# Where the stages of a two-layer encoder meet: splits, loads and waits by chunk and tile, and one pipeline across the turn

## The reference

```
h = rms_norm(x, norm_mix_pre[l]);  z = h @ w_in[l]              # 10 parts, 6144 columns
a = hgrn2_mixer(...);  b = diff_attention(...)                  # 512 columns each
m = sigmoid(gate_a) * (a @ w_branch_a[l]) + sigmoid(gate_b) * (b @ w_branch_b[l])
x = x + rms_norm(m @ w_out[l], norm_mix_post[l])
f = conv_ffn(rms_norm(x, norm_ffn_pre[l]), w_up[l], ...)        # 5632 columns up, 2816 down
x = x + rms_norm(f, norm_ffn_post[l])
x = x + rms_norm(sigmoid(rms_unit(x) @ w_ple_gate[l]) * (p[l] @ w_ple[l]), norm_ple[l])
```

## Time and profile before

| | |
|---|---|
| median of 3 runs | 2769.68 us |
| the profiled execution, its own time | 2770.27 us |
| its span | 2768.5 us |
| TensorE (PE) busy | 2635.0 us, 95% |
| VectorE (DVE), ScalarE (ACT), GpSimd (POOL) | 1478.4, 1063.6, 192.1 us |
| mean granted TensorE clock | 0.979 |

### The profile page before, as it was taken

The page is one execution under the profiler, slowest core; times in us unless marked ns, Lnnn a source line. Parts: engine busy times, 40 slices in busy tenths (PEclk is TensorE's granted clock), DMA queues, the critical chain, the costliest instruction groups (busy, mean ns, idle before and its releaser), DMA issues.

```text
span 2768.5 us, 36209 instructions
## 1 busy us (share of the span) xinstructions
PE 2635.0 (95%) x14994; PEld 2276.9 (82%) x14994; DVE 1478.4 (53%) x1836; ACT 1063.6 (38%) x1595; POOL 192.1 (7%) x272
## 2 busy tenths in 40 slices
PE   6999999999899999999979999999998999999998
PEld 5888988887688888887768889888776888888876
DVE  3166664444544444877442665743445444558774
ACT  3344453333332322455333544532333333234553
POOL 0001110000100000002111011100001000000021
PEclk9999999999899999999989999999998999999999
DMA  5534433344322222533235334333343222225321
GB/s 172 150 112 126 117 117 101 107 141 150 102 56 62 72 66 61 196 106 120 84 105 164 100 126 126 114 110 115 130 146 99 61 61 61 61 68 203 140 89 54
DMA packets 276222, 301.17 MB, mean 109 GB/s; under 512 B 9184, under 2 KB 210016, under 8 KB 276064
## 3 DMA queue, kind: packets, MB, share of 16 engines
q1 hardware_dynamic: 212192, 162.29, 19.6%
q10 hardware_dynamic: 63872, 136.64, 14.4%
HBM read 243.85 MB, written 55.05 MB: 108 GB/s over the span
## 4 chain that ended last, share of the span: by engine, by line
PE 87%; DVE 6%; ACT 3%; issue 2%; ACTq 1%; POOL 1%; DMA 0%; POOLq 0%; SPq 0%; DVEq 0%
PE ps L600 32%; PE ps L783 23%; PE ps L884 9%; PE ps L988 5%; PE ps L776 3%; PE ps L684 3%; PE ps L613 2%; PE ps L629 2%; PE ps L743 2%; PE ps L762 1%; PE ps L722 1%; PE ps L968 1%; PE ps L649 1%; PE ps L753 1%; DVE O L1231 1%
## 5 line engine op out<-in xcount | busy, mean ns | idle before, releaser
L600 PE MATMUL ps<-hT_hi,whi 128*128 128x256 f32 (+1 forms) x1664 | 428.0, 339 | 12.8 <-DVE hT_lo L1274 8.7
L600 PE MATMUL ps<-hT_hi,wlo 128*128 128x256 f32 (+1 forms) x1664 | 427.3, 338 | 0.0
L600 PE MATMUL ps<-hT_lo,whi 128*128 128x256 f32 (+1 forms) x1664 | 426.0, 337 | 0.0
L1061 DVE TENSOR_TENSOR wlo<-raw,whi 128x2048 fp32r<-128x2048 f32 x116 | 266.7, 2299 | 264.9 <-ACT whi L1559 264.9
L600 PEld LDWEIGHTS ps<-hT_hi,whi 128*128 128x128 f32 x1664 | 315.1, 190 | 50.5 <-issue 14.1
L600 PEld LDWEIGHTS ps<-hT_hi,wlo 128*128 128x128 f32 x1664 | 315.5, 190 | 37.3
L600 PEld LDWEIGHTS ps<-hT_lo,whi 128*128 128x128 f32 x1664 | 315.1, 189 | 37.0
L783 PE MATMUL ps<-hT_hi,whi 128*128 128x256 f32 (+1 forms) x1280 | 333.0, 342 | 5.0 <-ACT gst L1652 4.4
L783 PE MATMUL ps<-hT_hi,wlo 128*128 128x256 f32 (+1 forms) x1280 | 328.1, 338 | 0.0
L783 PE MATMUL ps<-hT_lo,whi 128*128 128x256 f32 (+1 forms) x1280 | 327.5, 338 | 0.0
L783 PEld LDWEIGHTS ps<-hT_lo,whi 128*128 128x128 f32 x1280 | 241.1, 188 | 28.7
(11 more groups left out here) (232 smaller groups left out, 4371.4 us busy)
## 6 DMA issues: line engine op xcount, KB each, us to landing
raw<-w_up_dram SPq DMA_DIRECT2D x88, 512.0 KB
raw<-w_in_dram SPq DMA_DIRECT2D x64, 512.0 KB
raw<-w_down_dram SPq DMA_DIRECT2D x60, 512.0 KB, 4.0
raw<-w_in_dram SPq DMA_DIRECT2D x16, 1024.0 KB
zT<-hn ACTq DMA_DIRECT2D x40, 384.0 KB, 2.9
zT<-gst ACTq DMA_DIRECT2D x40, 384.0 KB, 2.3
GT<-zT ACTq DMA_DIRECT2D x16, 768.0 KB, 5.6
FZ<-zT ACTq DMA_DIRECT2D x8, 1152.0 KB, 6.9
```

The source lines that it names most:

```text
L600: ins = mm(ps[:, bank, 0:tn], W[b][:, s, w0:w0 + P], rhs[a][:, k, t0:t0 + tn], start=(i == 0), stop=(i == n - 1))
L1061: v.tensor_tensor(wlo[:, s, :], raw[:, s, :], whi[:, s, :].bitcast(F32), ALU.subtract)\
```

## The change

The loads at the start are put in another order (x tile 0, identity, x tile 1, unit 0, the other tiles, the constants), the row loads come first on ScalarE, and the tables of constants are made after the first norm. The next layer's row loads are issued before the gate stage. A second norm block `hn2` is laid over O2 and gst1; tiles take turns. Squares write into it rather than elsewhere, after the transposes of the tile two before. The first unit is multiplied tile by tile, two transposes ahead. At the turn, norm and transposes of the next layer run within the last gate columns. Four of the eight blocks of mixer outputs are split before the last copy out; two gate loads are issued in the last head's mixer. The output projection waits for `mT_lo` by chunk and for the banks by tile. The second half of it, the transposes and six parts of the first up unit are put in one list; the first two up units are split within the norm stage. The loops of two rounds are written out. Cut to its core (unchanged lines, renamings and the moved constants' code left out):

SyncE, the start and the loops:

```diff
+    first_x(0)
+    sp.dma_start(ident[:], ident_in).then_inc(id_ld, 16)
+    first_x(1)
...
+                    if (L, j) == (0, 0):
+                        for t in range(2, NT):
+                            first_x(t)
+                        for dst, src in ((lamb[:, 0:2 * DEPTH * 2 * DA_DH], lam_in.partition_broadcast(P)), (lbl[:], lb_logits),
+                                         (X[:, 0, 0:NL * P], masks_in)):
+                            sp.dma_start(dst, src).then_inc(const_ld, 16)
-                with sp.Fori(0, 2) as i:
+                for i in range(2):
```

TensorE: the signal in the last gate unit (`project`), the first unit by tiles, the waits of the output projection, the list of the second half, the last gate columns:

```diff
                 if half:
                     ins.then_inc(z_mid if b == 0 else w_used, 1)
+                elif gate and b and w[0] % N_UNITS == N_IN - 1:
+                    ins.then_inc(z_last, 1)
...
+                def first_tile(t):
+                    if t == 0:
+                        unit_ready(unit(L, 0))
+                    if L:
+                        pe.wait_ge(pg_act.sem, pg_act.at(L - 1, f"s1_{t // 2}"))
+                    pe.wait_ge(n1["dve"].sem, n1["dve"].at(L, f"lo{t}_1"))
+                    token_tile(unit(L, 0), t, ((0, 1), (2, 3)))
+                if L == 0:
+                    norm_transposes(n1, L, tiles=(0, 1), buffers=hw)
+                for t in range(NT):
+                    first_tile(t)
+                    if t + 2 < NT:
+                        norm_transposes(n1, L, tiles=(t + 2,), buffers=hw)
...
-                pe.wait_ge(br_dve.sem, br_dve.last(L * 2 + 1))
+                def m_ready(k):
+                    pe.wait_ge(br_dve.sem, br_dve.at(L * 2 + k // 4, f"ml{k % 4 // 2}_{k % 2}"))
...
+                                 lambda t: pe.wait_ge(br_dve.sem, br_dve.at(L * 2 + 1, f"tb11_{t // 4}")), m_ready)
...
+                def up_part(b, t0, tn, bank, at):
+                    w = unit(L, U_UP)
+                    if (b, t0) == (0, 0):
+                        unit_ready(w)
+                    pe.wait_ge(nr["dve"].sem, nr["dve"].at(L, f"lo{(t0 + tn) // P - 1}_1"))
+                    pe.wait_ge(nr["dve"].sem, nr["dve"].at(L, f"ra{bank}"))
...
+                A, B, TURN, UP = range(4)
+                for what, n in ((A, 0), (A, 1), (B, 0), (B, 1), (A, 2), (B, 2), (A, 3), (TURN, 0), (B, 3), (A, 4), (TURN, 1), (A, 5),
+                                (B, 4), (TURN, 2), (B, 5), (UP, 0), (TURN, 3), (UP, 1), (UP, 2), (TURN, 4), (UP, 3), (TURN, 5), (UP, 4), (UP, 5)):
...
-                                (1, 0, 4), (1, 0, 5), (1, 1, 4), (1, 1, 5)):
+                                *(((1, 0, 4), (1, 1, 4), (1, 0, 5), (1, 1, 5)) if L == DEPTH - 1 else
+                                  ((None, 1, 0), (1, 0, 4), (1, 0, 5), (None, 1, 1), (1, 1, 4), (1, 1, 5)))):
```

VectorE (`first_scaled` scales into `hw[n % 2]`, `first_low` is the split after the transpose): the first norm, the second norm's two weight splits, the turn:

```diff
+                if L == 0:
+                    for i in range(NT + 1):
+                        if i < NT:
+                            first_scaled(L, i)
+                        if i:
+                            first_low(L, i - 1)
+                        if i == 1:
+                            low(unit(L, 0))
+                    low(unit(L, 1))
+                    constants()
...
-                norm_stage(nr, L, X, True, Y0w, lambda t: None, lambda s: low(unit(L, U_UP)) if s == NT else None)
+                norm_stage(nr, L, X, Y0w, lambda t: None, lambda s: low(unit(L, U_UP + (s == NT))) if s in (3, NT) else None)
...
+                for s in range(NT + (3 if following else 1)):
+                    if following and s == 4:
+                        low(unit(L + 1, 0))
                     if s < NT:
                         done(pg_act, L, f"s1_{s}")
                         v.tensor_tensor(E1[:, s, :], SG[:, s % 2, :], E1[:, s, :], ALU.mult).then_inc(*pg_dve.step(f"m1_{s}"))
-                    if s:
+                    if 1 <= s <= NT:
...
+                    if following and 2 <= s < NT + 2:
+                        first_scaled(L + 1, s - 2)
+                    if following and s >= 3:
+                        first_low(L + 1, s - 3)
+                    if following and s == NT:
+                        low(unit(L + 1, 1))
```

GpSimd makes the next layer's 1/rms of tile t behind the tail's of tile t + 1 (`first_rstd`). ScalarE: in the last head's mixer, at its end, the start and the turn (`layer_rows` are the four loads of row and layer constants):

```diff
+                else:
+                    unit_stored(L, N_IN - NH)
+                    done(A_pe, it, f"av{NT - 1}")
+                    done(G_pe, it, f"lv{NL - 1}")
+                    for b in range(2):
+                        load_gates(L, b)
...
+                    act.wait_ge(s_ab, L * 32 + 32)
+                    act.wait_ge(z_last, L + 1)
+                    for c in range(KD // 2):
+                        heads_high(L, c)
                     copy_out(L, N_IN - 1, 1, (6, 7))
                     store_out(L, N_IN - 1, 1)
...
+            layer_rows(0)
             for L in range(DEPTH):
+                if L == 0:
+                    for i in range(NT + 1):
+                        if i < NT:
+                            first_squares(L, i)
+                        if i:
+                            first_high(L, i - 1)
+                        if i == 1:
+                            high(unit(L, 0))
+                    high(unit(L, 1))
+                    act.wait_ge(const_ok, mark["exponents"])
...
                     if u == 4:
+                        if L == 0:
+                            act.wait_ge(const_ok, mark["all"])
...
                 row(wrows[:, 1, :], n_ple, L, s_wr)
+                if L + 1 < DEPTH:
+                    layer_rows(L + 1)
...
+                for s in range(NT + (3 if following else 2)):
+                    if following and s == 4:
+                        high(unit(L + 1, 0))
+                    if s < NT:
+                        gate_sigmoid(1, s)
+                    if 1 <= s <= NT:
+                        gate_square(1, s - 1)
+                    if following and 2 <= s < NT + 2:
+                        first_squares(L + 1, s - 2)
+                    if 2 <= s < NT + 2:
+                        store_last(s - 2)
+                    if following and s >= 3:
+                        first_high(L + 1, s - 3)
+                    if following and s == NT:
+                        high(unit(L + 1, 1))
```

More of the change, by code:

```diff
@@ L122, in norm_names, with first_names @@
                     "pe": [f"tr{n}_0", f"tr{n}_1"]}[engine]
+        if h >= 0:
+            out += {"act": [f"hi{h}_0", f"hi{h}_1"], "dve": [f"lo{h}_0", f"lo{h}_1"], "pool": [], "pe": []}[engine]
+    return out
+def first_names(engine):
+    out = []
+    for s in range(NT + 1):
+        n, h = s, s - 1
+        if n < NT:
+            out += {"act": [f"sqx{n}"], "dve": [f"hn{n}"], "pool": [f"mx{n}", f"rs{n}"], "pe": [f"tr{n}_0", f"tr{n}_1"]}[engine]
         if h >= 0:
@@ L603, in feature_block, with token_chunks @@
                 return ins
-            def token_chunks(lhs, s, chunks, first, last, counter, names, free=None):
+            def token_chunks(lhs, s, chunks, first, last, counter, names, free, ready):
                 for i, (w, k) in enumerate(chunks):
+                    ready(k)
                     for t in range(NT):
@@ L764, in att_values, with token_tile @@
                 ins.then_inc(*A_pe.step(f"av{q}"))
+            def token_tile(w, t, banks):
+                o = ps[:, (banks[0][0], banks[0][1], banks[1][0])[t // 2], (t % 2) * 256:(t % 2 + 1) * 256]
+                for k in range(KD):
+                    for i, (x, y) in enumerate(PASSES):
+                        ins = mm(o, hT[x][:, k, t * P:(t + 1) * P], view(W[y][:], w[2] * ISLOTS + k * P, [[1024, 2], [1, P]]),
+                                 start=(k == 0 and i == 0), stop=(k == KD - 1 and i == 2))
+                if t in (3, 5):
+                    ins.then_inc(z_mid if t == 3 else w_used, 1)
             def project(w, q, token, banks, gate=False):
@@ L844, in _ @@
                     mixers(L, h)
-                with pe.Fori(0, 2) as i:
+                for i in range(2):
                     it = L * 2 + i
@@ new lines, in wo_part @@
+                def wo_part(u, t):
+                    w = unit(L, U_WO + 2 + u)
+                    if u == 0:
+                        pe.wait_ge(wo_dve.sem, wo_dve.at(L, f"y{t}"))
+                    if t == 0:
+                        unit_ready(w)
+                    for k in range(4):
+                        for q, (a, b) in enumerate(PASSES):
+                            ins = mm(ps[:, t, :], mT[a][:, 4 * u + k, t * P:(t + 1) * P], W[b][:, w[2], k * 512:(k + 1) * 512],
+                                     start=(u == 0 and k == 0 and q == 0), stop=(u == 1 and k == 3 and q == 2))
+                    if t == NT - 1:
+                        ins.then_inc(w_used, 1)
+                    elif u:
+                        ins.then_inc(*wo_pe.step(f"a1_{t}"))
@@ L1263, in _ @@
                 v.tensor_scalar(sl_row[:], sl_row[:], lay_now[:, 1:2], None, ALU.mult).then_inc(*lay_dve.step("slw"))
-                for u in range(DENSE - 1):
-                    low(unit(L, u + 1))
+                for u in range(2, DENSE):
+                    low(unit(L, u))
```

(6 more changed lines are left out.)

329 lines of the change are left out of this document (173 added, 156 removed).

## The result

The changed kernel takes 2689.83 us (median of 4 runs, 2685.72 to 2690.98), the kernel before beside it 2769.1 (4 runs, 2765.17 to 2777.42): a ratio of 0.9707, 95% interval 0.9683 to 0.9732. The forecast was 2679.5, range 2662 to 2707. The profiled execution took 2690.98 us (span 2689.2); its gain on the profiled execution of before is 79.3 us, where 90.8 were forecast. The time lies in the range, but the miss of 11.5 us on the profiled execution has a cause that no rival named.

What follows compares the result with a forecast made beforehand. TensorE, busy 2635.0 of 2768.5 us, was taken to bound the kernel, shortened only at seams. Seam losses of 139.6 us falling to 48.8 save 90.8: 2770.3 becomes 2679.5 us, range 2662 to 2707.

Steps and rivals of the forecast that it cites:

- A: Seam from mixers to branch projections: 6.6 and 5.8 us lost in the two layers before, 0 forecast after.
- B: Seam from branch to output projection: 7.9 us lost in the first layer before, 0 forecast after.
- Rivals 2 to 5: Start held by weights, 2688 (0.08); clock stays low, 2813 (0.03); seams not opened, 2748 (0.04); more gained, 2660 (0.08).
- C: Output projection's second half to first up unit's end: 17.9 us lost before in layer one, 6.0 per layer forecast after.
- the hand layout: Hand-made schedule of output projection half tiles, transposes and first up unit parts, giving 4.8 us of stalls.
- U2: A sixth of the first up unit, forecast to wait 1.7 us for the low half of transposed tile 3.
- U4: A sixth of the first up unit, forecast to wait 2.5 us behind the second up unit's split.
- D: Turn between the layers: 28.3 us lost before, 9.2 forecast after, including 1.7 for the clock.
- E: Start of the kernel: 32.6 us lost before, 16.6 forecast after, with the first weights deciding.
- F: Tail after the last multiplication: 12.7 us before, 11.0 forecast after.
- Rival 1: Waits move to VectorE and POOL as slowed POOL steps come on the path: 2701 us, chance 0.22.
- rows 4: Profile rows giving TensorE's full pace: 0.35 us per pair of 256 and 512 columns, 0.227 us for 512.

Runs made afterwards that it cites:

- experiment 7: Changed kernel with all eight mixer outputs split after the last copy out of PSUM and gate loads issued where they were: 2706.39 us.
- experiment 8: Changed kernel with one wait for the whole of mT_lo put back before the output projection: 2705.62 us.
- experiments 8 to 11: Changed kernel with, in turn, one wait for mT_lo, old first-load order, second up unit's split earlier, single norm block: 2705.62, 2700.67, 2686.66, 2687.42 us.
- experiment 10: Changed kernel with the second up unit's copy and split moved ahead of those of transposed tile 4: 2686.66 us.
- experiments 1 to 5: Kernel before with the six parts alone: 2782.5 us; changed kernel with one, four, two unused transposes: 2688.17, 2681.66, 2677.87; with four 256-column products: 2693.26.
- experiments 6 to 8 and 11: Changed kernel with, in turn, TensorE's branch loop restored, old mixer-to-branch seam, one mT_lo wait, single norm block: 2693.72, 2706.39, 2705.62, 2687.42 us.
- experiment 12: Changed kernel with four unused transposes before the second up unit and dense unit 1 of each layer, and two weight splits moved: 2672.98 us, ratio 0.9629.

## Why the prediction was right or wrong

**Direction, and that the seams open: right.** The signs named for it all came: the waits on mT_lo and on the mixer outputs are gone, the clock in A and B is 1.00, dense unit 1 starts at 39.9 (forecast 39.3), the first up unit ends 60.8 us after the second half of the output projection begins (forecast 61.0 with the clock), and the turn's chain reaches unit 1 at 1373.6, 29.5 us after the end that the gate products had in the old order (forecast 30.2). Rivals 2 to 5 are out.

**A:** forecast loss 0, and 0 came. The gain was undercounted, since the cost before reached past the window I cut (experiment 7): 66.7 us for the branch products against 69.2 and 69.6. **B:** no loss is left, and experiment 8 gives the single wait's worth as 6.7 us in each layer, for the forecast's 7.9.

**C:** 55.0 us of work in 60.8 leaves 5.8 (forecast 6.0). That this fits is partly luck: the 1.2 for a fallen clock were not needed in the first layer, and the stalls are 4.6 (forecast 4.8); the other 1.2 are work that the sum had too low, such as 17.3 us for the six parts, taken at 16.9. The stalls stand where the hand layout had them: 0.8 before transpose 3 (forecast 0.5), 1.5 before U2 (1.7), 2.3 before U4 (2.5). The second layer took 62.3, a loss of 7.3: its clock fell once, which cost 1.5. In the kernels of experiments 8 to 11 it fell in neither layer. The cause named for U4, the second unit's split ahead of lo5, was right in part: with it moved, 0.7 of the 2.3 us went (experiment 10).

**D:** the gates begin at 1294.6 and unit 1 at 1373.6: 79.0 us, with 49.5 for the gates (as before) and 22.7 for transposes and tiles. The loss is 6.8, not 9.2. The first wait came as forecast (1.05 for 1.2), and VectorE was a little faster than laid out (the scalings of tiles 2 to 5 start 4.6 to 5.6 us apart; I had 5.9). The clock did not fall at all, so the 1.7 for it were not needed.

**E:** 17.2 us lost for 16.6. The transfer fits what was worked out: by 12.65 at the latest (forecast 11), and at 19.67 in the old order. The weights decide, as forecast: TensorE waits 2.0 us for their split, and the first products start at 16.94 (forecast near 15.8). **F:** 11.1 for 11.0.

**Rival 1, waits on VectorE and GpSimd:** it didn't decide. The slow POOL steps are there, and they aren't on the path. GpSimd's timeline at the turn, kernel after:
```profile
1346.18 0.19 POOL L1583 TENSOR_SCALAR msy<-msy 128x1 f32<-128x1 f32 x1 [0.20 <-POOL msy L1648]
...
1354.14 1.20 POOL L1648 TENSOR_TENSOR msy<-ssy 128x1 f32<-128x1 f32 x1 [1.65 <-ACT JK L2244]
1355.54 1.00 POOL L1583 TENSOR_SCALAR msy<-msy 128x1 f32<-128x1 f32 x1 [0.20 <-POOL msy L1648]
...
1357.25 0.19 POOL L1583 TENSOR_SCALAR msx<-ssx 128x1 f32<-128x1 f32 x1
```
VectorE's timeline beside it:
```profile
1355.21 1.28 DVE L1167 SCALAR_TENSOR_TENSOR hn<-XM,rsx,wrows 128x1024 f32<-128x1024 f32 x1
1356.41 1.28 DVE L1174 TENSOR_TENSOR hT_lo<-ps,hT_hi 128x512 fp32r<-128x512 f32 x2
```
The same operation takes 0.19 us where VectorE waits (1346.18) and 1.00 beside VectorE's scaling, whose two tiles XM and wrows both lie in SBUF. Beside the split, which reads one of its two from PSUM, it takes 0.19 again (1357.25). The Trainium skill (SBUF — State Buffer, Who interferes with whom, The single rule) has the two engines exclude each other over a shared port; the trace agrees in the durations. The time that the rival made of it (2701) did not come: TensorE's waits at the turn are the 1.05 to 1.6 us of the layout that left the slowed steps out.

**The step that failed** is one that the prediction did not write down: that the work outside the seams keeps its pace. It took the pair at 0.35 us from rows 4 for every pair, and counted the six parts at 24 x 0.12, nearly the sum of the old unit. The parts do cost that. But they change what precedes the other 21 units, and at 0.3533 us per pair for 0.3467 that is 13.4 us (experiments 1 to 5 tie it to the parts). The seams' surplus of 3.8 us hides a part of it, and the range of 45 us is wide enough for the rest, so that the time lies in the range says little about this step. The other -1.9 us are in the down projection and the tail before the turn, with 1.4 of them between the first layer's down projection and its gates, where the granted clock is 0.98 over 71 us (0.83 from 1265 to 1275) and was 1.00 in the kernel before. From the last product before that stretch to the first of the gates it is 72.1 us here, but 70.6 to 70.8 in the kernels of experiments 6 to 8 and 11, which share its code, and 70.7 in the kernel before. So such a fall comes in some executions and not in others, and nothing ties it to the change.

The trace of before held the sign. Its dense stage took 84.57 us for 240 pairs at full clock, 0.353 per pair, where the up stage's 1156 multiplications in 200 us make 0.346: a second pace for the same shapes, behind the very kind of stream that the change puts ahead of the up stage.

## What to carry to other kernels

A stage of one shape at full clock without waits is not at one pace for all that: count its multiplications over equal stretches in every stage before it is called untouched, since a change ahead of it can move all of it. Where a long alternating stream follows one of another shape, two or more small transposes between them are worth a try (here 0.13 us of them in each layer, for 6.6 us in each). And a seam's price reaches as far as the stage behind it is slower than its twin; cut the window at that stage's end.

## What was not expected of the hardware

- TensorE ran alternating products of 256 and 512 columns at one of two paces, 16.64 or 16.96 us per 96, at a granted clock of 1.00, with no change over 350 us. Direct entry of the up stage from products of 256 columns gave the slow one each time (both layers of eight kernels, one of them with four more such products, and of the kernel before with the parts); two or four 128-column transposes between gave the fast one, one transpose did not. The dense units show the same: 84.6 us in both layers of every kernel but that of experiment 12, and 83.1 there, with four transposes ahead of them.
- The slow pace isn't even: of three pairs in a row one takes 0.35 us and two near 0.36, as the starts 60.28, 60.64, 60.98, 61.34 and 61.70 in the dense stage of the kernel before show. In the fast pace each takes 0.35.
- It is no rule for all entries. The branch stage, entered directly from pairs of the gate units, is fast in both layers of the kernel after (233 multiplications in 40 us). Behind the 4.3 us wait of experiment 7 it is slow in the first layer and fast in the second:
```profile
590.00:630.00 40.00, 40.00 (x228) 34.63 (x228) 22.45 (x31) 14.16 (x11) 0.00 (x0) 1.00 0.39 131
1935.00:1975.00 40.00, 40.00 (x233) 34.97 (x232) 22.95 (x31) 13.77 (x11) 0.00 (x0) 1.00 0.39 132
```
In the kernel before, with the same wait, it is the other way round (232 from 605 to 645, 228 from 1980 to 2020). So a wait can end in either pace, and a part of what seam A cost was this. What in TensorE keeps the pace stays open: granted clock, waits and DMA share don't tell the two apart.
- One wait of 4.9 us was enough for a granted clock of 0.83 in the next 10 us (experiment 8), while three waits of 0.8, 1.5 and 2.3 us in the 61 us of C left it at 1.00 in the first layer and came with one low stretch, worth 1.5 us, in the second. The Trainium skill (TensorE: Matmul & The Clock Gate, A second HAM failure mode: psum-queue depth-cycling) tells of short idle spells between groups that make the clock swing; the rows of C show at most one such fall for three waits.
